# Router logits of the second half from un-normalised residual chunks; weight prefetch split around the first gather

## The chip, the cores and the metric

One core of one Trainium2 chip runs the whole program. The metric is the device time of one execution in microseconds (us), median over runs.

## The reference: one layer of a hybrid decoder

1024 prompt rows and 8 x 4 sample rows of width D = 1024 go through adaLN-modulated RMSNorm, a combined input projection, three mixers, an output projection with a gated residual add, and then a mixture of experts (32 experts, two for each row). Cut to what matters here:

```
x  = x + g1 * mixed                                   # mixed: the output projection's product
h2 = rms_norm(x, norm2_g) * (1 + sc2) + sh2           # A2 = norm2_g * (1 + sc2), B2 = sh2
g_logits = h2 @ w_router_g + b_router_g               # 4 groups
e_logits = h2 @ w_router_e + b_router_e               # 32 experts
# top-1 group, top-2 experts in it; rows sorted by expert, padded to blocks of 128
y = sum of weight * (silu(h2 @ w1[e]) * (h2 @ w3[e])) @ w2[e]
out = rms_norm(x + g2 * y, final_norm_g)
```

The prompt rows share one A2 and one B2, each sample sequence has its own. With r the inverse root mean square of a row, h2 @ W = r * ((x * A2) @ W) + B2 @ W.

## The kernel before: two halves, a routing step, 33 expert blocks

**Dense stage.** Rows are worked in two halves, g = 0 (512 prompt rows) and g = 1 (512 prompt rows and 32 sample rows, five tiles t = 0 to 4). PE's products are *items* (`item(g, i, ...)`), one for each 128 columns of output, with three f32r matmuls for each 128 rows of weights (high by high, low by high, high by low). The last eight items of a half are the output projection (`out_item`). Each gives 128 columns of the result with tokens along the free dimension; `out_transpose` turns them back, and DVE's `out_add` adds them to the residual `xres`.

**Order.** All of it is written out by hand: each engine has one program, with semaphores between them. Nothing is scheduled by a tool.

**The tail of half 0** is woven into half 1: `tail_h2(0, t)` on DVE makes h2 rows, PE transposes them (`h2_transpose`), ACT copies (`tail_tile`), PE's `logits` multiplies eight chunks by the router's 36 columns.

**The tail of half 1** stands by itself, since nothing dense is left: DVE waits for ACT's sums of squares of all eight chunks (`x1_sq`), makes r (`tail_start`), and makes h2 of the five tiles; for each tile PE transposes eight chunks (`last_transpose`), ACT copies them (`last_tile`), PE multiplies (`last_logits`), DVE adds the bias. GpSimd (POOL) writes rows of x1 and h2 to DRAM through its own queue. 44 matmuls on `ident` whose result nobody reads run ahead of it on PE.

**Routing** (`moe_vector`, `moe_tensor`) is a chain of small DVE instructions on the logits. `oh_ok` says that the experts are chosen; PE's rank matmuls follow (behind 30 matmuls of `keep_busy`), then DVE makes the list of rows of each expert (`tok_ok`), and POOL gathers the first block of h2 rows out of DRAM (`gather(0)`).

**Experts.** 33 blocks (`NB`), each of 128 gathered rows. A block takes six weight chunks of 1 MB (`CHUNKS`: four of w1 and w3, two of w2), which SP loads into a ring of `RN` = 13 buffers. ACT rounds a chunk (`high`, `whr`), DVE makes the rest (`low`, `wl`), PE multiplies (`up`, `Y`); `T` transposes gathered rows, `G` the hidden ones. ACT applies a sigmoid (`sigm`), and DVE two products (`gate_one`, `gate_two`). Load n waits until chunk n - 13 has been multiplied (`m_c`). `dense_done` holds an engine until all the dense stage's rows are in DRAM; SP, POOL, ACT and DVE each wait there.

Of the kernel before, what the change touches and what calls it, by code (L numbers as in the profile page):

```python
# [74 lines left out]
N_CONST = 14  # L75
# [3 lines left out]
def build(nc, x_prompt, x_sample, c_prompt, c_sample, state_conv_a, state_conv_c, norm1_g, norm2_g,  # L79
# [5 lines left out]
    with ctx:  # L85
# [7 lines left out]
        y_dram = nc.dram_tensor("y_rows", (2 * TPAD, D), F32, kind="Internal").ap()  # L93
        table = nc.dram_tensor("slot_table", (NBLK * P * NE, 1), I32, kind="Internal").ap()
# [60 lines left out]
        w_hi = [sb(f"w_hi{s}", [P, KD, P], F32R) for s in range(WS)]  # L155
        a_in = sb("a_in", [P, CW, HA + HALF + NS * AS])
# [10 lines left out]
        cv_end = top[0]  # L167
        p_in = sb("p_in", [P, HC + HALF + NS * CS])
# [9 lines left out]
        wsT = sb("wsT", [P, HEADS, P])  # L178
        wsS = sb("wsS", [SMP, HEADS, SMP])
        s_bias = sb("s_bias", [P, CW, P])  # L180
# [19 lines left out]
        rw = sb("rw", [P, KD, NR])  # L200
        rb = sb("rb", [P, NR])
        assert top[0] <= nc.sbuf_usable_end, top[0] - nc.sbuf_usable_end

        h2s, h2T, sqd = [None] * (PT + 1), [None] * 2, [None] * 2
        h2s[0], o = at("h2s0", [P, D], F32, act0_at)
        h2T[0], o = at("h2T0", [P, KD, P], F32, o)
        A2, o = at("A2", [P, D], F32, o)
# [4 lines left out]
        h2T[1], _ = at("h2T1", [P, KD, P], F32, macc_at)  # L212
# [14 lines left out]
        sp8, o = at("sp8", [P, PT + 1, KD], F32, vT_at)  # L227
# [109 lines left out]
        id_ok, sz_ok, az_ok, wsr_ok = (sem(n) for n in ("id_ok", "sz_ok", "az_ok", "wsr_ok"))  # L337
# [4 lines left out]
        x0_in = [sem(f"x0_in{t}") for t in range(PT)]  # L342
# [18 lines left out]
        vT_ok, vn_ok, v_out = sem("vT_ok"), sem("vn_ok"), sem("v_out")  # L361
# [8 lines left out]
        h2_last = [sem(f"h2_last{s}") for s in range(2)]  # L370
        ab_in, abs_in = sem("ab_in"), sem("abs_in")
        h2_ok, h2_out, x1_out = sem("h2_ok"), sem("h2_out"), sem("x1_out")
        hT_ok, hT_rd, lg_ok, lg_rd = sem("hT_ok"), sem("hT_rd"), sem("lg_ok"), sem("lg_rd")
# [22 lines left out]
        def lg_bank(t):  # L396

            return (q[1], z[1])[t % 4 // 2][:, t % 2, :]
# [45 lines left out]
        for g in range(2):  # L444
            if g:
                for i in range(PT):
                    use(0, "h2T", 0, i), use(1, "lg", 0, i)
# [4 lines left out]
            if g:  # L452
                use(0, "stA"), use(1, "stC")
            for c in range(CW):
                use(c % 2, "mu", g, c)
            use(1, "var", g)
            for c in range(CW):
                use(c % 2, "bc", g, c)
# [5 lines left out]
        use(0, "h2T", 1), use(1, "lg", 1)  # L464
# [53 lines left out]
        def x_dump(g):  # L518
# [3 lines left out]
        xs_s = conv_flat[0:SMP, :]  # L522
# [13 lines left out]
        m_T, m_xT, m_xl, m_sg, m_g1, m_g2, m_G, m_gT, m_gl, m_y = (  # L536
            sem(n) for n in ("m_T", "m_xT", "m_xl", "m_sg", "m_g1", "m_g2", "m_G", "m_gT", "m_gl", "m_y"))
        o_i, o_w, o_c, o_x, o_sc = (sem(n) for n in ("o_i", "o_w", "o_c", "o_x", "o_sc"))
        f_in = [sem(f"f_in{s}") for s in range(NT)]
# [3 lines left out]
        f_rows = [P] * (NT - 1) + [SMP]  # L543

# [15 lines left out]
        def dense_done(eng):  # L560

            eng.wait_ge(item_mm, 2 * NI)
            eng.wait_ge(h2_last[0], 16 * ((PT + 2) // 2))
            eng.wait_ge(h2_last[1], 16 * ((PT + 1) // 2))
            eng.wait_ge(x1_out, 16 * NT)
            eng.wait_ge(x1_sq, PT + KD * (PT + 1))
            q_wait_read(eng, "lg", 1)
# [21 lines left out]
        def moe_sync(sp):  # L589
# [7 lines left out]
            for n in (0, 1, 2, 3, 8):  # L597
                load(n, CHUNKS[n][0])
            dense_done(sp)
            for n in (4, 5, 6, 7, *range(9, 10 * RN)):  # L600
                load(n, CHUNKS[n][0])
# [39 lines left out]
            for t in F_ORDER:  # L641
                for k in range(2):
                    r0 = t * P + k * TPAD
                    sp.dma_start(yin[0:f_rows[t], t, k, :], y_dram[r0:r0 + f_rows[t], :]).then_inc(f_in[t], 16)
# [6 lines left out]
        def moe_gpsimd(pool):  # L651
            dense_done(pool)
            pool.memset(xg[0][:], 0.0).then_inc(xg0_ok, 1)
            pool.drain()
            pool.memset(xg[1][:], 0.0).then_inc(xg0_ok, 1)
# [1093 lines left out]
        def _(dve):  # L1749
# [557 lines left out]
            for t in range(PT):  # L2307
                tail_h2(1, t)
# [367 lines left out]
```

## Time and profile before

| | us |
|---|---|
| median of 3 runs | 1684.01 |
| lowest and highest run | 1677.58, 1684.67 |
| profiled execution | 1686.75 |
| its span | 1685.0 |
| mean granted clock of TensorE | 0.974 of full speed |

The span is what the trace covers; 1.75 us of the profiled execution lie outside it. Times in the rows below count from the span's start. PE is the matmul engine, DVE the vector engine, ACT the scalar engine, SPq the queue of SyncE that issues loads. A chain step is `start us, duration us, what`, where `what` is the engine, the tile written and the line.

### The profile page before, as it was taken

Reading aid. Unit: us, or ns where it says so; the run is one execution under the profiler, and the core shown is the slowest. Engines: PE = TensorE matmul, PEld = TensorE weight load, DVE = VectorE, ACT = ScalarE, POOL = GpSimd, SP = SyncE. Lnnn points to the kernel's source line nnn. Section 1 sums busy time; section 2 is a strip of 40 time slices with the busy share of each in tenths; the row PEclk is TensorE's granted clock in tenths of the full one; section 3 lists DMA queues with packets and bytes.
Section 4 is the critical chain, followed back from the end, with each engine's and each line's share of the span. In section 5 each row is a group of like instructions: output and inputs, shape, how many; then the busy total and the mean of one; then the engine's idle time right before and its main releaser. Section 6 shows DMA issues by size and latency. Waiting matters only on the chain.

```text
span 1685.0 us, 23762 instructions
## 1 busy us (share of the span) xinstructions
PE 1606.8 (95%) x9382; PEld 1386.0 (82%) x9382; DVE 1259.1 (75%) x1691; ACT 805.0 (48%) x875; POOL 244.7 (15%) x239
## 2 busy tenths in 40 slices
PE   5999999999999999999999998999999999999953
PEld 3776788788789999999999996888888888888841
DVE  3668886756839798967454268989989999899847
ACT  4222232244432223222333434887878878878722
POOL 2310000000000000002002012355321221212200
PEclk9999999999999999999999978999999999999987
DMA  9965223424434322324134347999999999999865
GB/s 340 303 201 158 78 88 89 137 76 144 128 99 147 91 86 69 97 79 133 58 94 131 152 175 236 409 390 398 383 379 377 384 367 388 375 388 395 308 231 191
DMA packets 215761, 368.51 MB, mean 219 GB/s; under 512 B 15110, under 2 KB 163654, under 8 KB 190298
## 3 DMA queue, kind: packets, MB, share of 16 engines
q1 hardware_dynamic: 197724, 327.95, 55.1%
q0 software_dynamic: 17280, 36.89, 6.1%
q10 hardware_dynamic: 646, 2.15, 0.3%
q8 instruction: 75, 1.23, 0.3%
q14 instruction: 36, 0.29, 0.0%
HBM read 353.45 MB, written 31.20 MB: 228 GB/s over the span
## 4 chain that ended last, share of the span: by engine, by line
PE 85%; DVE 7%; DMA 2%; DVEq 2%; issue 1%; ACT 1%; POOL 0%; SPq 0%; POOLq 0%; ACTq 0%
PE z L2428 15%; PE z L2430 15%; PE z L2429 15%; PE z L723 7%; PE z L725 7%; PE z L724 7%; PE z L740 4%; PE z L742 4%; PE z L741 4%; PE q L714 2%; PE q L2321 1%; DMA ada_h<-in_w_ada_dram 1%; PE q L2340 1%; PE q L731 1%; DVE conv L1919 1%
## 5 line engine op out<-in xcount | busy, mean ns | idle before, releaser
L973 DVE TENSOR_TENSOR wl<-wr,whr 128x2048 fp32r<-128x2048 f32 x198 | 444.2, 2284 | 0.0
L2428 PE MATMUL z<-h_hi,w_hi 128*128 128x272 f32 (+1 forms) x1248 | 410.2, 329 | 2.7 <-issue 1.2
L2430 PE MATMUL z<-h_hi,w_lo 128*128 128x272 f32 (+1 forms) x1248 | 404.6, 324 | 0.0
L2429 PE MATMUL z<-h_lo,w_hi 128*128 128x272 f32 (+1 forms) x1248 | 403.9, 324 | 0.0
L881 ACT ACTIVATE whr<-wr 128x2048 fp32r<-128x2048 f32 x198 | 376.3, 1914 | 37.9 <-PE z L725 32.2
L1751 DVE TENSOR_TENSOR w_lo<-w_raw,w_hi 128x1024 fp32r<-128x1024 f32 (+1 forms) x168 | 179.5, 1069 | 143.3 <-ACT w_hi L1483 143.3
L2428 PEld LDWEIGHTS z<-h_hi,w_hi 128*128 128x128 f32 x1248 | 236.8, 190 | 31.9 <-issue 13.7
L2430 PEld LDWEIGHTS z<-h_hi,w_lo 128*128 128x128 f32 x1248 | 236.3, 189 | 17.1
L2429 PEld LDWEIGHTS z<-h_lo,w_hi 128*128 128x128 f32 x1248 | 236.7, 190 | 15.7 <-issue 0.2
L723 PE MATMUL z<-whr,xTh 128*128 128x512 f32 x528 | 209.9, 398 | 2.4 <-DVE xTl L973 2.4
L725 PE MATMUL z<-wl,xTh 128*128 128x512 f32 x528 | 207.1, 392 | 0.0
L724 PE MATMUL z<-whr,xTl 128*128 128x512 f32 x528 | 206.5, 391 | 0.0
L1919 DVE SCALAR_TENSOR_TENSOR conv<-a_in,parT,conv 128x512 f32<-128x512 f32 x360 | 193.7, 582 | 14.1 <-issue 0.9
L1483 ACT ACTIVATE w_hi<-w_raw 128x1024 fp32r<-128x1024 f32 (+1 forms) x168 | 150.3, 929 | 46.0 <-DMA w_raw<-in_w_in_dram 45.9
L1652 ACT ACTIVATE sig<-z 128x512 f32<-128x512 f32 (+1 forms) x48 | 29.3, 611 | 287.6 <-PE z L2430 287.6
L669 POOL DMA_INDIRECT y_rows<-ysb,tb x32 | 93.2, 2911 | 392.0 <-ACT ysb L873 392.0
L723 PEld LDWEIGHTS z<-whr,xTh 128*128 128x128 f32 x528 | 100.2, 190 | 22.4 <-DVE xTl L973 2.8
L725 PEld LDWEIGHTS z<-wl,xTh 128*128 128x128 f32 x528 | 99.7, 189 | 21.4
L724 PEld LDWEIGHTS z<-whr,xTl 128*128 128x128 f32 x528 | 99.9, 189 | 19.8
L740 PE MATMUL z<-whr,gTh 128*128 128x512 f32 x264 | 105.8, 401 | 0.4 <-DVE gTl L973 0.4
L742 PE MATMUL z<-wl,gTh 128*128 128x512 f32 x264 | 103.1, 391 | 0.0
L741 PE MATMUL z<-whr,gTl 128*128 128x512 f32 x264 | 103.0, 390 | 0.0
(378 smaller groups left out, 2240.8 us busy)
## 6 DMA issues: line engine op xcount, KB each, us to landing
wr<-in_w_dram SPq DMA_DIRECT2D x198, 1024.0 KB, 7.9
w_raw<-in_w_in_dram SPq DMA_DIRECT2D x104, 512.0 KB, 3.8
ada<-in_w_ada_dram SPq DMA_DIRECT2D x6, 2048.0 KB, 14.2
w_raw<-in_w_branch_dram SPq DMA_DIRECT2D x48, 256.0 KB, 2.7
w_raw<-in_w_out_dram SPq DMA_DIRECT2D x16, 512.0 KB, 3.8
yin<-y_rows SPq DMA_DIRECT2D x16, 512.0 KB, 10.0
ada_h<-in_w_ada_dram SPq DMA_DIRECT2D x2, 2048.0 KB, 15.2
ada_u<-in_w_ada_dram SPq DMA_DIRECT2D x2, 2048.0 KB, 10.0
```

Of the source, the lines that this page charges most:

```text
L723: pe.matmul(out, xTh[s][:, k, :], hi[:, i * FF:(i + 1) * FF], start=(k == 0), stop=False)
L724: pe.matmul(out, xTl[s][:, k, :], hi[:, i * FF:(i + 1) * FF], start=False, stop=False)
L725: last = pe.matmul(out, xTh[s][:, k, :], lo[:, i * FF:(i + 1) * FF], start=False, stop=(k == KD - 1))
L740: pe.matmul(out, gTh[:, k, :], hi[:, w0:w0 + 512], start=(k == 0), stop=False)
L742: last = pe.matmul(out, gTh[:, k, :], lo[:, w0:w0 + 512], start=False, stop=(k == KF - 1))
L881: act.activation(whr[n % HN][:], wr[n % RN][:], ACT.Copy).then_inc(m_hi, 1)
L973: return dve.tensor_tensor(out, a, b, op)
L1751: return dve.tensor_tensor(out, a, b, op)
L1919: last = dve.scalar_tensor_tensor(out, x, wt, out, ALU.mult, ALU.add)
L2428: pe.matmul(out, w_hi[w][:, k, :], hi[:, k, t0:t1], start=(k == 0), stop=False)
L2429: pe.matmul(out, w_hi[w][:, k, :], lo[:, k, t0:t1], start=False, stop=False)
L2430: last = pe.matmul(out, w_lo[w][:, k, :], hi[:, k, t0:t1], start=False, stop=(k == kn - 1))
```

## The change

Nine things are done.

1. The logits of half 1 are no longer taken from h2. PE transposes chunks of `xres` as each becomes ready (`x1_columns`), ACT multiplies by A2 (a column) while copying, and PE multiplies the router's columns (padded to 64) as the stationary side by 512 rows at once (`x1_scores`); even chunks write PSUM partitions 0 to 63, odd ones 64 to 127. `last_rows` turns the result back and adds the two halves. DVE multiplies by r and adds a bias that includes B2 @ W (`last_scores`). The samples go the same way in small (`sample_scores`).
2. The h2 rows of half 1 are made in place in `xA` (= xres * A2, made by `x1_scale` between the output items): three tiles by DVE, and the last prompt tile and the sample tile by PE (`h2_product`), read by ACT.
3. The eighth chunk's squares move from ACT to DVE; the other seven are taken before the last item ends.
4. `out_transpose(1, 3, 0)` moves into the middle of the last output item, and the 44 idle matmuls go; `keep_busy` ahead of the rank goes from 30 to 26.
5. SP writes x1 and h2 of half 1, in place of POOL. Its h2 writes wait until its x1 writes have landed.
6. The weight chunks: 0 to 4 are loaded early, where it was 0 to 3 and 8; then 5, 6 and 12 when the last item is done; 7 to 11 wait for the first gather to land, where eight chunks were issued at `dense_done`.
7. Half 0's logits are made by the same method in one go (`first_columns`, `first_rows`) in place of four times eight products.
8. `factor_columns`, `shift_scores` and `shift_rows` bring A2 as columns and B2 @ W, in half 1's dense stage.
9. Experts: Silu on ACT and one DVE product (`gate`) take the place of the sigmoid and two products. DVE no longer waits at `dense_done`, but for `he_ok` behind `oh_ok`.

The core of the diff:

```diff
@@ moe_sync
-            for n in (0, 1, 2, 3, 8):
+            for n in range(5):
                 load(n, CHUNKS[n][0])
+            sp.wait_ge(item_mm, 2 * NI)
+            for n in (5, 6, 12):
+                load(n, CHUNKS[n][0])
+            sp.wait_ge(xa_ok, KD)
+            for t, rows in tiles(1):
+                r0 = (PT + t) * P
+                sp.dma_start(x1_dram[r0:r0 + rows, :], xres[0:rows, t, :]).then_inc(last_out[t % 2], 16)
...
             dense_done(sp)
-            for n in (4, 5, 6, 7, *range(9, 10 * RN)):
+            sp.wait_ge(m_xg[0], 16)
+            for n in (7, 8, 9, 10, 11, *range(13, 10 * RN)):
                 load(n, CHUNKS[n][0])
@@ moe_tensor
-            keep_busy(pe, 30)
+            keep_busy(pe, 26)
             s = q_wait_free(pe, "rank")
+            pe.wait_ge(he_ok, PT + 1 - NH_D)
@@ moe_vector
-            dense_done(dve)
...
             last.then_inc(oh_ok, 1)
+            dve.wait_ge(he_ok, PT + 1 - NH_D)
...
-            def gate_one():
-                tt(gs[:], hsg[:], z[0][:, 0, :], ALU.mult).then_inc(m_g1, 1)
-
-            def gate_two():
-                tt(gs[:], gs[:], z[0][:, 1, :], ALU.mult).then_inc(m_g2, 1)
+            def gate():
+                tt(gs[:], hsg[:], z[0][:, 1, :], ALU.mult).then_inc(m_g2, 1)
@@ scalar engine, end of the dense stage
+            q_wait_read(act, "mc")
+            for c in range(KD):
+                x1_read(c)
+            x1_read_samples()
+            scores_read(1)
+            act.wait_ge(r_ok, 1)
+            for t, rows in tiles(1)[NH_D:]:
+                act.activation(hdg[0:rows, t - NH_D, 0:rows], ident[0:rows, 0:rows], ACT.Copy,
+                               scale=r2y[0:rows, t:t + 1]).then_inc(hd_ok, 1)
+            for t, rows in tiles(1)[NH_D:]:
+                act.wait_ge(xc_ok, KD + 1 + t - NH_D + 1)
+                act.activation(xA[0:rows, t, :], h2_bank(t)[0:rows].rearrange("p b c -> p (b c)"), ACT.Copy).then_inc(he_ok, 1)
@@ vector engine, end of the dense stage
             tail_start(1)
-            for t in range(PT):
-                tail_h2(1, t)
-            dve.wait_ge(abs_in, 16 * 2 * NS)
-            tail_h2(1, PT, SMP, (xs_s[:, D:2 * D], xs_s[:, 0:D]))
-            for t, rows in tiles(1):
-                tail_logits(1, t, rows)
+            for t in range(NH_D):
+                dve.scalar_tensor_tensor(xA[:, t, :], xA[:, t, :], r2y[:, t:t + 1], B2[:], ALU.mult, ALU.add).then_inc(h2_ok, 1)
+            last_scores()
@@ tensor engine
+            def column_scores(out, x, c, first, last):
+
+                r = 64 * (c % 2)
+                return pe.matmul(out[r:r + NRP], rw[:, c, :], x, start=first, stop=last)
...
+            def h2_product(t, rows):
...
+                for h in range(2):
+                    out, cc = h2_bank(t)[0:rows, h, :], slice(512 * h, 512 * h + 512)
+                    pe.matmul(out, ident[0:rows, 0:rows], shift[0:rows, cc], start=True, stop=False)
+                    last = pe.matmul(out, hdg[0:rows, t - NH_D, 0:rows], xA[0:rows, t, cc], start=False, stop=True)
```

PE before, behind the last output item (`ot` is the output item's result, `h2s` the h2 rows, `h2T` their transposes, `rw` the router's columns):

```order
L2321 MATMUL q<-ident,ot_110 128x128 x4
L2321 MATMUL q<-ident,ot_110 32x128
L2321 MATMUL q<-ident,ot_111 128x128 x4
L2321 MATMUL q<-ident,ot_111 32x128
L2644 MATMUL z<-ident 128x128 x44
L2321 MATMUL q<-ident,h2s_141 128x128 x8
L2321 MATMUL z<-ident,h2s_148 128x128 x8
L2473 MATMUL q<-rw,h2T_142 128x36 x8
L2321 MATMUL q<-ident,h2s_149 128x128 x8
L2473 MATMUL q<-rw,h2T_147 128x36 x8
```

The same place in the changed kernel, from the first transposes behind the last item to the matmuls ahead of the rank (`x1T` are the transposed chunks, `LT` the logits with tokens along the free dimension, `both` a matrix that adds the halves, `B_148` the shift B2):

```order
L2449 MATMUL q<-ident,xres 128x128 x8
L2573 MATMUL z<-x1T,rw 64x512 x2
L2449 MATMUL z<-ident,xres 128x128 x8
L2449 MATMUL q<-ident,xA 128x32 x8
L2573 MATMUL z<-x1T,rw 64x512 x4
L2573 MATMUL z<-x1T,rw 64x32 x8
L2577 MATMUL q<-both,LT_143 128x36 x4
L2577 MATMUL q<-both,LT_143 32x36
L2645 MATMUL z<-B_148,ident 128x512
L2646 MATMUL z<-xA,hdg 128x512
L2645 MATMUL z<-B_148,ident 128x512
L2646 MATMUL z<-xA,hdg 128x512
```

The transposes of h2 and the 36-column products are gone; chunks of `xres` are transposed instead, and products for h2 rows now stand behind the logits.

SP in the changed kernel, from the last of the five early chunks on, with the semaphores that it waits for:

```order
L621 DMA wr_193<-in_w_dram 128x2048
L621 DMA wr_211<-in_w_dram 128x2048 [waits item_mm]
L621 DMA wr_213<-in_w_dram 128x2048
L621 DMA wr_207<-in_w_dram 128x2048
L639 DMA x_rows<-xres 128x1024 [waits xa_ok]
L651 DMA h_rows<-xA 128x1024 [waits last_out0,last_out1,x1_sq,h2_ok,xc_ok,r_ok]
L651 DMA h_rows<-xA 128x1024 [waits he_ok]
L651 DMA h_rows<-xA 32x1024 [waits he_ok]
L621 DMA wr_215<-in_w_dram 128x2048 [waits h2_ok,he_ok,x1_sq,h2_out,x1_out,lg_rd,last_out1,m_xg0,last_out0,item_mm]
```

Between the weight loads there now stand ten writes of rows; before, SP's list had weight loads alone here, and the writes were in POOL's.

## Rows read from the trace of the kernel before

**Rows 1.** The page's part 4: the chain that ended last, by engine.

```profile
PE 85%; DVE 7%; DMA 2%; DVEq 2%; issue 1%; ACT 1%; POOL 0%; SPq 0%; POOLq 0%; ACTq 0%
```

**Rows 2.** The chain in order of time: from the last output item to block 2.

```profile
968.15 0.14 PE z L2430
969.37 0.79 DVE xres L1751 x2
974.71 0.19 DVE ssq L1965
978.02 1.28 DVE h2s L1941
...
1002.89 0.37 DVE m8g L996 x4
...
1020.80 5.88 DMA xg<-h_rows,tok
1026.93 1.96 PE q L714 x8
...
1031.25 0.79 PE z L723
...
1070.26 0.88 PE q L714 x8
1088.01 0.88 PE q L714 x8
```

**Rows 3.** Stretches: busy us (and instructions) of each engine, granted clock, DMA share.

```profile
970.00:972.00 2.00, 1.79 (x16) 1.78 (x17) 1.83 (x5) 1.81 (x13) 0.00 (x0) 1.00 0.00 0
986.00:988.00 2.00, 2.00 (x11) 2.00 (x11) 1.93 (x2) 0.00 (x0) 0.94 (x2) 0.50 0.97 377
1006.00:1008.00 2.00, 2.00 (x21) 2.00 (x19) 1.74 (x12) 2.00 (x2) 0.00 (x0) 1.00 1.00 414
1200.00:1300.00 100.00, 100.00 (x473) 83.77 (x473) 90.84 (x56) 80.28 (x57) 24.33 (x12) 1.00 0.99 377
```

**Rows 4.** Timeline of PE from the last item to the rank.

```profile
970.21 0.77 PE L2321 MATMUL q<-ident,ot 128*128 128x128 f32 x5 [1.39 <-DVE xres L1751]
970.81 9.99 PE L2644 MATMUL z<-ident 128*128 128x128 f32 x88
1002.06 8.79 PE L748 MATMUL z<-ident 128*128 128x128 f32 x60
1011.85 0.18 PE L760 MATMUL q<-ohs,tri 128*128 128x32 bf16 x1 [1.01 <-issue]
```

**Rows 5.** The chain: steps on PE elsewhere.

```profile
50.81 1.85 PE q L2340 x16
322.42 1.72 PE q L2583 x4
350.49 1.90 PE q L2603 x32
522.91 1.71 PE q L2445 x16
```

**Rows 6.** Timeline of ACT: a table load, then rounding of three chunks.

```profile
1010.01 1.28 ACT L889 ACT_TABLE_LOAD   x1
...
1011.44 5.49 ACT L881 ACTIVATE whr<-wr 128x2048 fp32r<-128x2048 f32 x3
```

**Rows 7.** Groups of instructions from 900 to 1055 us: count, busy, mean ns.

```profile
L1751 DVE TENSOR_TENSOR xres<-q,xres 128x512 f32<-128x512 f32 x8 | 5.4, 669 | 0.0
```

**Rows 8.** DMA issues from 905 to 1060 us: KB each, median us to landing.

```profile
wr<-in_w_dram SPq DMA_DIRECT2D x21, 1024.0 KB, 9.7
h_rows<-h2s POOLq DMA_DIRECT2D x4, 512.0 KB, 4.5
```

**Rows 9.** Gathers of rows (tile xg) from 1000 to 1100 us.

```profile
DMA to landing us min/median/max: 4.1/5.9/11.9
```

**Rows 10.** Waits in SP's queue from 1100 to 1600 us: total us, times, longest.

```profile
SPq L587 <- PE z L725: 272.3, 109, 2.9
```

More of the change, by code:

```diff
@@ L341, in build @@
         bada_in = [sem(f"bada_in{s}") for s in range(2)]
-        x0_in = [sem(f"x0_in{t}") for t in range(PT)]
+        rows_in = [sem(f"rows_in{t}") for t in range(NT)]
         x_in = [sem(f"x_in{s}") for s in range(5)]
@@ L2411, in _, with item @@
             pe.wait_ge(xt_free, PT)
-            def item(g, i, hi, lo, split_ok=None):
+            def item(g, i, hi, lo, split_ok=None, between=None):
                 u, s, w, kn = i // 2, i % 2, (NI * g + i) % WS, w_cols(i)
@@ L2421, in item @@
                     [(part, k) for part in parts for k in range(kn)]
-                for (b, t0, t1), k in steps:
+                for n, ((b, t0, t1), k) in enumerate(steps):
+                    if between and n == kn:
+                        between()
                     out = z[s][:, b, 0:t1 - t0]
@@ L2477, in out_item, with row_scores, first_columns @@
-            def out_item(g, j, s):
+            def column_scores(out, x, c, first, last):
+                r = 64 * (c % 2)
+                return pe.matmul(out[r:r + NRP], rw[:, c, :], x, start=first, stop=last)
+            def row_scores(out, g, t, rows):
+                return pe.matmul(out[0:rows, t * NR:(t + 1) * NR], LT[g][:, t * P:t * P + rows], both[:], start=True, stop=True)
+            def first_columns():
+                pe.wait_ge(consts, N_CONST)
+                pe.wait_ge(par2_in, 16 * N_PAR2)
+                q_wait_read(pe, "h2T", 0, PT - 1)
+                q_wait_free(pe, "vT", 1, 0)
+                for c in range(KD):
+                    last = column_scores(q[1][:, 0, :], h2T[:, c, :], c, c < 2, c >= KD - 2)
+                last.then_inc(lt_ok, 1)
@@ new lines, in first_rows, with x1_columns @@
+            def first_rows():
+                pe.wait_ge(ltc_ok, 1)
+                for t in range(PT):
+                    last = row_scores(q[1][:, 1, :], 0, t, P)
+                last.then_inc(lg_ok, 1)
+            def x1_columns(c):
+                pe.wait_ge(xa_ok, c + 1)
+                if c == 0:
+                    q_wait_read(pe, "oT", 1, KD - 2)
+                elif c == 1:
+                    pe.wait_ge(z_free[1], NI)
+                elif c == 3:
+                    q_wait_read(pe, "oT", 1, KD - 1)
+                elif c >= 5:
+                    pe.wait_ge(xe_ok, c - 4)
+                for t in range(PT):
+                    last = transposed(x1_bank(c)[:, t * P:(t + 1) * P], xres[:, t, c * P:(c + 1) * P])
+                last.then_inc(xc_ok, 1)
@@ new lines, in factor_columns, with shift_scores @@
+            def factor_columns():
+                s = q_wait_free(pe, "mc")
+                pe.wait_ge(mc_in, 32)
+                transposed(q[s][:, 0, 0:P], bn_g[:, 0:P])
+                transposed(q[s][:, 0, P:9 * 2 * KD], bn_g[0:2 * KD, P:2 * P]).then_inc(q_ready[s], 1)
+            def shift_scores():
+                s = q_wait_free(pe, "sc")
+                q_wait_read(pe, "mc")
+                for c in range(KD):
+                    last = column_scores(q[s][:, 0, 0:9], abT[:, :, 0, c], c, c < 2, c >= KD - 2)
+                last.then_inc(q_ready[s], 1)
@@ L2638, in _ @@
                     out_transpose(g, j - 1, 1)
-                    out_item(g, j, 1)
-                if g:
-                    out_transpose(g, KD // 2 - 1, 0)
-                    out_transpose(g, KD // 2 - 1, 1)
-            for _ in range(44):
-                pe.matmul(z[1][:, 0, 0:P], ident[:], ident[:], start=True, stop=True)
-            for t, rows in tiles(1):
-                last_transpose(t, rows)
-                if t:
-                    last_logits(t - 1, P)
-            last_logits(PT, SMP)
+                    if g and j == KD // 2 - 1:
+                        out_item(g, j, 1, between=lambda: out_transpose(1, KD // 2 - 1, 0))
+                    else:
+                        out_item(g, j, 1)
+            x1_columns(0)
+            out_transpose(1, KD // 2 - 1, 1)
+            for c in (1, 2, 3):
+                x1_columns(c)
+            x1_scores(0)
+            x1_columns(4)
+            x1_columns(5)
+            x1_scores(1)
+            x1_columns(6)
+            x1_columns(7)
+            x1_samples()
+            x1_scores(2)
+            x1_scores(3)
+            sample_scores()
+            last_rows()
+            for t, rows in tiles(1)[NH_D:]:
+                h2_product(t, rows)
             moe_tensor(pe)
```

412 lines of the change are left out of this document (259 added, 153 removed).

## The prediction

> **What bounds the kernel now.** I read the chain that ended last first: PE has 85% of it, DVE 7% [rows 1]. Then the chain in order of time. An expert block starts each 17.75 us (1088.01 - 1070.26), and in such blocks PE is busy 100 of 100 us at full clock, DVE 90.8, ACT 80.3 [rows 2, 3]. So the experts are bound by PE, the change gives PE no less to do there, and what it saves on DVE (one product a block) lies beside PE's work: nothing. The dense stage is PE's too. The place where the engines take turns lies between them: the last dense matmul ends at 968.3 (I call this E), the chosen experts are looked for from 1002.89, the first gather is issued at 1020.80, its transposes begin at 1026.93, the first expert matmul at 1031.25 [rows 2]. From E to T(0) that is 58.6 us, while an expert's matmuls need 17.75 us a block; what shortens these 58.6 us comes off the end, as all behind stays in order.
>
> Where they go: E to r ready (978.02), 9.7 us; h2, transposes and logits of five tiles to 1002.89, 24.9 us; routing to the gather 17.9 us; the gather 5.9 us [rows 2]. In the second piece PE worked at half its clock: granted 0.50 from 986 to 988, busy 2.00 of 2 us, after 1.00 at 970 to 972 and again at 1006 to 1008 [rows 3].
>
> **The change, step by step, in us after E, at full clock.** Three chains have to be followed.
>
> *Logits by way of DVE.* DVE is free of the output at +1.1 (969.37) and PE's five transposes take 0.8 (they waited for DVE's earlier sums before, which now come earlier) [rows 2, 4]: +1.9. The sum over four tiles and the samples' own, two instructions at or below 0.67 [rows 7]: +2.8. The eighth chunk's squares, now on DVE: product, reduction and their sample parts, four instructions by 0.67 at most, with the x1 scale ahead, I take 2.2: +5.0. From there to the rows of h2 it took 3.3 (974.71 to 978.02) [rows 2]: +8.3. The last x1 scale 0.7, then three of the four-column kind of instruction that took 1.28 [rows 2]: +12.8. The bias and r on the logits, five small ones, no row: between 0.5 and 2, I take 1.0, as they are far smaller than the 0.67 ones: **+13.8**, where 1002.89 was +34.6.
>
> *Logits by way of PE.* Transposing eight chunks of four tiles is 32 transposes; 16 f32 instructions of a similar size take about 1.9 at most [rows 5], so 3.6; five for the output 0.8; samples and the small products about 2.4. The eight products of 512 columns have no row. A 128-wide one cost 0.86 (four instructions, two products, 1.72); with four strips side by side an instruction cost 0.116 (1.85 / 16), and with two strips, 128 columns, 0.059 (1.90 / 32), against 0.114 (9.99 / 88) for the full width [rows 4, 5]. So two strips run beside each other: 0.43 each, bounds 0.23 and 0.86, the sum 3.4 (1.9 to 6.9). With the wait for the output at the start PE ends the logits at about +11.5, behind DVE's rows only: DVE decides. At 0.86 each PE ends at +15, and all below is 2 us later.
>
> *PE on to the rank.* Behind the logits stand the h2 products of two tiles, eight by 0.86 (the sample tile has 32 rows, but the same 512 columns): 6.9, +18.4. 26 idle matmuls are 52 instructions by 0.114: 5.9, so the rank can start at **+24.3**. DVE reaches the rank's input 9.0 us after its start (1011.85 - 1002.89), +22.8 [rows 2, 4]. So PE is 1.5 us late there, of which DVE hides about 0.4. From the rank to the transposes it was 15.1 (1026.93 - 1011.85). The gather took 5.9 while weight loads filled the DMA (share 1.00 at 1006); the quickest of the gathers took 4.1 [rows 3, 9]. Nothing is loaded now ahead of it, so I take 1.8 off; the bounds are 0 and, if the shortest one still met others, 3. T(0) is then at 24.3 + 15.1 - 0.4 - 1.8 = **+37.2**, where it was +58.6: 21.4 less.
>
> *Rows in DRAM and ACT behind them.* ACT still waits for all rows in DRAM, then needs 5.5 for three chunks, a table load of 1.3 with three small ones, and 5.5 again, say 12.8, before it takes T(0)'s result [rows 6]. SP: three chunks (3 MB; some 380 GB/s, [rows 3]) to about +9, x1 rows 2.1 MB to +14.5, and only then h2. The last tile is read at +19.5 and lands by +23 (a row write took 4.5 [rows 8]). ACT is through at +36, T(0) is done at +39. It fits by 3 us. If the landing is 4 us later, ACT sets the pace.
>
> *What is held back.* Chunks 7 to 11 start when the gather lands. A load lands 9.7 after issue in this stretch [rows 8] and the next follow at 2.8 (1.05 MB at 377 GB/s): 7 at T(0) + 10, then 13, 16, 19, 21. Before, PE's first block took until about T(0) + 19, and chunk 7 is multiplied in the second. In steady blocks SP waits for PE 109 times from 1100 to 1600 us, 272 us in all [rows 10], so there is room to catch up. Nothing.
>
> *The dense stage.* Half 0's logits cost 4 x 1.71 [rows 5]; now eight by 0.43 and four small ones of 0.2 each, 4.3: -2.5. A2's columns and the shift's logits: about 1.7, and 0.4 for a bank that ACT must read first. The transposes inside the last item: +0.6. Sum +0.2, bounds -2 and +4.
>
> **The clock** is what I know least. PE goes without ordinary matmuls from E to about +3.4: transposes and waits alone. Before, the clock held over the pause at 970 (idle 1.39, then 1.00) but then fell and stayed at 0.50 while PE was busy with transposes and products of 36 columns, and it rose within 4 us of ordinary matmuls (1002.06 to 1006) [rows 3, 4]. So a fall near +4 is likely, and the products of 512 columns may lift it again; I take half-speed for 3.5 us, that is 1.7 lost. The Trainium skill, "TensorE: Matmul & The Clock Gate", Part 4, says that a PE transpose does not count as PE being busy. By that rule the clock stays low until the products of 512 columns weigh more than the transposes, which is the second rival below; the trace agrees in so far as the clock stayed at 0.50 where half of PE's work was transposes, but its other half was of 36 columns, so it can't tell the two apart.
>
> **The sum:** -21.4 + 1.7 + 0.2 = -19.5. The profiled execution (1686.75, span 1685.0) would become 1667.2. It lies 2.7 above the median of the runs, so I set the difference against the median: 1684.0 - 19.5 = **1664.5**.
>
> **Rivals.**
>
> *Clock low up to the h2 products.* PE's logits after +4 then take twice as long: about +17.3 (some of it is waiting, which the clock doesn't stretch), DVE +18.4; the products, low for their first 3.9, take 8.9, +26.2; 5.9 idle ones, rank at +32; T(0) at +44.9. Saved 13.7, time **1670.5**. For it: [rows 3]'s 0.50. Against: here products of 512 columns stand in between, from +3.4 on. 22%.
>
> *Clock low all the way, or rows late in DRAM.* Logits +20.3 to +21.4, products 13.8, idle ones 11.8: rank at +46, T(0) at about +59. Time **1684**; or, at full clock, h2 landing 10 us later, which puts ACT at +46: 1674. For the clock: nothing shows that f32 products with 64 of 128 columns used lift it. Against: in [rows 4], [rows 3], f32 matmuls on `ident` did lift it, and the h2 products are as wide. 13% for this group, a third of it within 0.5%, or 8.4 us, of no change, which is about what a measurement of this kernel can tell.
>
> *Slower: Silu brings table loads into each block.* A load costs 1.28 [rows 6]. If Silu and the copies of rounding don't share a table, two loads stand in each block, 2.56 us. ACT has 3.5 us to spare in a block of 17.75 (80.3 of 100), but hidden rows, rounded chunks and T's result all pass through it in turn, so a part shows on PE. It decides above 19.5 / 32 = 0.6 us a block; one load shown is 41 us, time **1705**. Against: at 1010.01 one load stood ahead of the exponential, and the three copies behind it had none [rows 6]. 5%.
>
> *Nothing gained,* since a new wait takes it back (the bank of `mc`, chunks too late, or DVE's waits): **1682**, 7%.
>
> **How the numbers follow.** Forecast 50% (own range 1658 to 1668), first rival 22%, second 13%, Silu 5%, nothing 7%, and 3% for more gain than 27 us, if PE is warm when the first block starts. Range **1657 to 1677**: it leaves out the 5, the 7, the 3 and part of the 13. Faster by over 0.5%: 50 + 22 + 3 + some 8 of the 13 = 0.83. Within 0.5%: 0.11. Slower: 0.06.
>
> **What would show it.** The choice of experts begins at E + 14 (over + 18: the clock; look at the granted clock from E to + 12). The rank starts at + 24 and waits for PE's idle matmuls, not DVE. The gather takes 4.1 or less. ACT is through with its sixth chunk ahead of T(0). Expert blocks keep 17.75 us, without a table load in them, and no ACT wait for chunks 7 to 11. Wrong it would be if ACT or `he_ok` ends the wait at the rank or at T(0), or if the blocks lengthen.

## The result, and the profile of the changed kernel

The changed kernel took 1669.35 us (median of 5 runs, 1666.21 to 1672.21) where the kernel before, on the same chip, took 1679.51 (5 runs, 1677.58 to 1684.67): ratio 0.9936, 95% interval 0.9912 to 0.9960. Five later runs of it had a median of 1669.43. Forecast was 1664.5 in 1657 to 1677, and "faster". So the sign and the range held, but of a gain of 19.5 us only 10.2 came.

The chain by engine, from the page, to be held against [rows 1]: PE has a point more, DVE a point less.

```profile
PE 86%; DVE 6%; DMA 2%; DVEq 2%; ACT 1%; issue 1%; POOL 0%; SPq 0%; POOLq 0%; ACTq 0%
```

The chain in order of time between the last dense matmul and block 2, which answers to [rows 2]. E, the end of the last dense matmul, is 969.2 here.

```profile
970.60 0.75 PE q L2449 x5
...
977.71 1.89 PE z L2573 x8
...
981.53 1.06 PE z L2645 x2
...
989.12 8.83 PE z L803 x52
999.10 0.46 DVE oh L1030
...
1006.37 5.41 DMA xg<-h_rows,tok
...
1012.03 1.96 PE q L769 x8
...
1016.34 0.79 PE z L778
...
1055.27 0.88 PE q L769 x8
1073.02 0.88 PE q L769 x8
```

The reader sees that DVE's long turns of before ([rows 2], 974.71 to 1002.89) are out of the chain, and that PE holds it from 971 to 998. T(0), the first transpose of gathered rows, is at E + 42.8 (1012.03) and was at E + 58.8 (the forecast's 58.6 counts from another end of the same matmul, see the table below). The blocks behind still lie 17.75 us apart.

PE's timeline from E to the rank, to be held against [rows 4]:

```profile
972.95 1.08 PE L2573 MATMUL z<-x1T,rw 128*64 128x512 f32 x4
...
980.27 1.26 PE L2577 MATMUL q<-both,LT 128*128 128x36 f32 x10 [0.26 <-ACT LT L1619]
981.47 1.13 PE L2645 MATMUL z<-B,ident 128*128 128x512 f32 x2
...
985.10 1.04 PE L2645 MATMUL q<-xs_s,ident 32*32 32x512 f32 x2
...
987.70 1.42 PE L2646 MATMUL q<-xA,hdg 32*32 32x512 f32 x2
989.05 8.90 PE L803 MATMUL z<-ident 128*128 128x128 f32 x52
997.78 0.18 PE L816 MATMUL q<-ohs,tri 128*128 128x32 bf16 x1
```

The logits end at E + 12.3, the h2 products at E + 19.9, and then come the 52 instructions of `keep_busy`, at 0.171 us each instead of 0.114. The stretches say why, the granted TensorE clock being the third number from the end (columns as in [rows 3]):

```profile
970.00:972.00 2.00, 1.40 (x13) 1.39 (x13) 0.82 (x3) 1.00 (x3) 0.37 (x1) 1.00 0.78 217
986.00:988.00 2.00, 2.00 (x6) 0.51 (x5) 1.77 (x12) 0.23 (x1) 0.00 (x0) 1.00 0.03 8
990.00:992.00 2.00, 2.00 (x12) 2.00 (x11) 1.64 (x8) 0.17 (x1) 0.00 (x0) 0.50 1.02 395
1006.00:1008.00 2.00, 2.00 (x20) 2.00 (x20) 1.75 (x2) 2.00 (x2) 1.63 (x1) 1.00 0.00 0
1018.00:1020.00 2.00, 2.00 (x6) 1.52 (x6) 1.83 (x7) 0.00 (x0) 0.00 (x0) 0.50 1.00 416
1200.00:1300.00 100.00, 100.00 (x472) 83.71 (x471) 87.80 (x51) 81.34 (x56) 21.01 (x12) 1.00 0.98 376
```

The clock stayed at full through the logits, fell to half (1.2 of 2.4 GHz) only at 988.2, in the last of the products of the sample tile, which use 32 rows and 32 columns of the array, and again under the first block, behind PE's pause at the gather. In the steady stretch DVE lost the 3 us in 100 that the second product cost (90.84 in [rows 3]), and PE's 100 of 100 shows that this is worth nothing.

ACT waits for the rows of h2 and then rounds, beside [rows 6]:

```profile
995.71 5.51 ACT L937 ACTIVATE whr<-wr 128x2048 fp32r<-128x2048 f32 x3 [5.54 <-DMA h_rows<-xA]
...
1001.43 1.28 ACT L945 ACT_TABLE_LOAD   x1
...
1002.86 5.50 ACT L937 ACTIVATE whr<-wr 128x2048 fp32r<-128x2048 f32 x3
```

It is through at 1008.4, 3.7 us ahead of T(0).

### The profile page after: what moved, and what is told of

Its sections match the earlier page's. It is cut to its first block, busy times and chain, and to the rows that moved or that the text cites. A ratio compares the mean times of both kernels' runs of the same rounds, so it can differ in the third digit from the quotient of the medians.

```text
span 1670.5 us, 23444 instructions
## 1 busy us (share of the span) xinstructions
PE 1595.8 (96%) x9246; PEld 1362.9 (82%) x9246; DVE 1243.1 (74%) x1666; ACT 807.9 (48%) x876; POOL 216.0 (13%) x236
## 4 chain that ended last, share of the span: by engine, by line
PE 86%; DVE 6%; DMA 2%; DVEq 2%; ACT 1%; issue 1%; POOL 0%; SPq 0%; POOLq 0%; ACTq 0%
PE z L2558 15%; PE z L2560 15%; PE z L2559 15%; PE z L778 7%; PE z L780 7%; PE z L779 7%; PE z L795 4%; PE z L797 4%; PE z L796 4%; PE q L769 2%; PE q L2449 1%; DMA ada_h<-in_w_ada_dram 1%; PE q L2468 1%; PE q L786 1%; DVE conv L1994 1%
## 5 line engine op out<-in xcount | busy, mean ns | idle before, releaser
L937 ACT ACTIVATE whr<-wr 128x2048 fp32r<-128x2048 f32 x198 | 376.4, 1914 | 38.4 <-PE z L780 32.6
L724 POOL DMA_INDIRECT y_rows<-ysb,tb x32 | 78.2, 2443 | 418.0 <-ACT ysb L929 418.0
```

What stands on the lines that cost most here:

```text
L937: act.activation(whr[n % HN][:], wr[n % RN][:], ACT.Copy).then_inc(m_hi, 1)
```

## Experiments

All edits are to the changed kernel, where nothing else is said. Ratios are to the kernel before, run on the same chip; the changed kernel's own is 0.9936. Most edits are smaller than what runs of one kernel differ by, so the traces are set side by side first, and each is read from its own E:

| trace | E | rank, from E | gather, us | T(0), from E | 2nd block, from E |
|---|---|---|---|---|---|
| before | 968.1 | 43.7 | 5.88 | 58.8 | 71.2 |
| b1, before again | 965.5 | 43.7 | 6.13 | 59.0 | 71.4 |
| b2, before again | 965.6 | 36.0 | 7.05 | 52.3 | 64.1 |
| e8, before, loads held | 965.6 | 36.0 | 5.57 | 50.8 | 63.2 |
| changed | 969.2 | 28.6 | 5.41 | 42.8 | 55.5 |
| a1, changed again | 968.6 | 25.4 | 5.56 | 39.8 | 52.0 |
| e1 | 969.2 | 25.0 | 5.44 | 39.3 | 52.0 |
| e2 | 969.0 | 22.9 | 5.49 | 38.4 | 49.5 |
| e3 | 966.7 | 27.0 | 7.80 | 43.6 | 56.0 |
| e4 | 970.0 | 27.0 | 5.50 | 41.3 | 53.6 |
| e5 | 966.9 | 23.0 | 5.50 | 37.5 | 50.1 |
| e6 | 969.0 | 23.0 | 5.62 | 37.6 | 46.7 |
| e7 | 966.9 | 25.4 | 5.52 | 39.7 | 50.9 |
| e9, e6 again | 969.3 | 23.0 | 5.54 | 37.5 | 46.6 |

(Rank: its first matmul starts. Gather: its step in the chain. T(0): first transpose of gathered rows. 2nd block: the first transpose of its rows. E, the end of the last dense matmul, is taken here as the start of its row in the timeline and 0.13 us, the distance at which such matmuls follow each other; the row's own end, 968.3 in before, lies 0.15 later, and the forecast's 58.6 counts from there.)

**e1: the sample tile's products over the whole array.** Its rows of h2 are left out.

```diff
-out = h2_bank(t)[0:rows, h, :]
-pe.matmul(out, ident[0:rows, 0:rows], shift[0:rows, cc], ...)
-pe.matmul(out, hdg[0:rows, t - NH_D, 0:rows], xA[0:rows, t, cc], ...)
+out = h2_bank(t)[:, h, :]          # for t == PT
+pe.matmul(out, ident[:], B2[:, cc], ...)
+pe.matmul(out, ident[:], B2[:, cc], ...)
```

> The changed kernel, but the four matmuls that make the sample tile's h2 rows (32 rows and 32 columns of the array, 512 moving columns) are replaced by four of 128 rows and 128 columns with the same 512 moving columns, on other data; the h2 rows of the samples are therefore left out of the result, the logits are as before. Theory A: the granted clock falls to 0.50 behind the logits (989 to 995 in the changed kernel) because the sample tile's product leaves most of the array idle. Then the clock stays at 1.00 through this stretch, the 52 idle-matmul instructions ahead of the rank take about 5.9 us in place of 8.8, the rank starts about 3 us sooner after the last dense matmul, and so does the first expert transpose, unless the rows' landing holds it. Rival C: the fall comes from the transposes and waits right behind the dense stage, late by some delay; then the low stretch stays and nothing moves.

Measured: 1667.66 (1666.63 to 1668.61), ratio 0.9922 (0.9896 to 0.9948). PE's timeline in e1:

```profile
987.56 1.02 PE L2652 MATMUL q<-B,ident 128*128 128x512 f32 x2
988.42 5.97 PE L803 MATMUL z<-ident 128*128 128x128 f32 x52
994.22 0.18 PE L816 MATMUL q<-ohs,tri 128*128 128x32 bf16 x1
```

The 52 idle instructions take 5.97 us, which is the forecast's 5.9, and the rank stands at E + 25.0. With as many products of as many columns, spread over the whole array, the clock stayed up in this trace. That doesn't yet show that the small ones make it fall: a1 below has the small ones and no fall either, so this single trace decides neither for theory A nor against rival C.

**e2: four idle matmuls instead of 26.**

```diff
-            keep_busy(pe, 26)
+            keep_busy(pe, 4)
```

> The changed kernel with 4 idle matmuls ahead of the rank in place of 26. Theory A: PE holds the rank (DVE sat idle 5.5 us for it in the changed kernel), so the rank starts as soon as the experts are chosen, 5 to 5.5 us sooner, and the first expert matmul 4 to 5.5 us sooner; total 4 to 5 us less than the changed kernel, less what a lower clock at the first blocks costs (up to 2). Rival B: the landing of the h2 rows and ACT's six roundings behind it set the first block; ACT was through at 1008.4 and took the first transposes' result at 1014.0, so then the gain ends at 5.6 minus the sooner rank, or stops outright if the gather itself waits for the rows: at most 1 to 2 us.

Measured: 1665.78 (1665.17 to 1666.53), ratio 0.9913 (0.9887 to 0.9939). PE's timeline:

```profile
988.97 2.07 PE L803 MATMUL z<-ident 128*128 128x128 f32 x8
991.98 0.18 PE L816 MATMUL q<-ohs,tri 128*128 128x32 bf16 x1 [0.94 <-DVE ohs L1088]
...
993.61 5.56 PE L803 MATMUL z<-ident 128*128 128x128 f32 x28
```

The rank now waits for DVE, at E + 22.9; the forecast had DVE there at + 22.8. So PE held the rank, and neither ACT nor the landing of h2 did. The clock is low here too, so the next 28 idle instructions take 5.56 instead of 3.39, and part of the 5.7 us is given back.

**e3: chunks 7 to 11 not held for the gather.**

```diff
-            sp.wait_ge(m_xg[0], 16)
```

> The changed kernel, but weight chunks 7 to 11 are loaded once all rows are in DRAM, without waiting for the first gather. My forecast took 1.8 us for the emptier DMA during the gather; the profile of the changed kernel shows 5.41 where it was 5.88. If contention costs what the two profiles show, the gather's step in the chain is 5.4 to 6 us here and the total differs by under 1 us. Rival: the hold is what keeps the gather quick, and without it the gather step grows by 1.8 or more and all behind it with it. Chunks 7 to 11 are early in either case.

Measured: 1668.69 (1667.49 to 1671.81), ratio 0.9932 (0.9910 to 0.9954). The chain's row of the gather in e3:

```profile
1002.24 7.80 DMA xg<-h_rows,tok
```

The hold is worth 2.4 us of the gather, and from the rank to T(0) it took 16.6 us where it was 14.3. The medians (0.7 us apart, and not the way of the trace) can't show it: five runs of either kernel lie 4 to 6 us apart, and this trace's own E is 2.5 us earlier.

**e4: SP writes h2 without waiting for x1 to land.**

```diff
-            sp.wait_ge(last_out[0], 16 * ((PT + 2) // 2))
-            sp.wait_ge(last_out[1], 16 * ((PT + 1) // 2))
```

> The changed kernel, but SP writes the h2 rows without first waiting until its x1 writes have landed. Theory: that wait held the h2 writes from 981 to 988 (issue at 988.0) and all rows' landing to 995.7; without it the landing comes at 992 to 993 (the sample tile is read by ACT at 990.2), ACT is through with six chunks at about 1005.5, and since nothing of this is on the chain (the rank is), the first expert matmul and the total stay within 1 us. Rival B: the landing is on the chain by way of ACT or of the gather; then the first block starts about 3 us sooner.

Measured: 1668.04 (1666.74 to 1672.24), ratio 0.9931 (0.9909 to 0.9954). ACT's rounding:

```profile
993.66 5.51 ACT L935 ACTIVATE whr<-wr 128x2048 fp32r<-128x2048 f32 x3 [3.10 <-DMA h_rows<-xA]
```

It begins at E + 23.7 where it was E + 26.5, and T(0) did not follow: from the rank to T(0) it took 14.3 us in both. The rows' landing is not on the chain there.

**e7: the sigmoid and two products back in the blocks.** The waits that go with them, and the place of the two products in DVE's order, change too and are left out here.

```diff
-act.activation(hsg[:], z[0][:, 0, :], ACT.Silu)...
+act.activation(hsg[:], z[0][:, 0, :], ACT.Sigmoid)...
-tt(gs[:], hsg[:], z[0][:, 1, :], ALU.mult)...
+tt(gs[:], hsg[:], z[0][:, 0, :], ALU.mult)...
+tt(gs[:], gs[:], z[0][:, 1, :], ALU.mult)...
```

> The changed kernel with the expert blocks of before: a sigmoid on ACT and two products on DVE. Forecast: nothing, as a block stays 17.75 us with DVE at 90 of 100 us. Rival: the one product less on DVE was on the chain in the first two blocks, and the total grows by 0.7 to 1.4 us (too small for the total, but the distance from the first block's transposes to the third's shows it).

Measured: 1669.94 (1664.97 to 1670.88), ratio 0.9948 (0.9933 to 0.9964). From T(0) to the fourth block it took 41.9 us, in the changed kernel 43.1 (85.9 - 42.8) and in a1 42.8. The trace gained 1.2 rather than lost, at the first block's clock; the medians can't be told apart. Behind the first block, where the clock is full in all traces, there is a small difference: from the second block's transposes to the fourth's it took 30.72 to 30.75 us in the five traces with the sigmoid (before, b1, b2, e8, e7) and 30.41 to 30.60 in the nine with Silu. So Silu gives 0.1 to 0.3 us once, less than the expectation's rival had, and nothing that the times can tell. It brought no table loads: one load stands in the first block of either.

**b1 and b2: the kernel before, unchanged, once each; a1: the changed kernel again.**

> The kernel before, unchanged, for a second trace. Its profiled execution had a span of 1685.0 us at a mean granted clock of 0.974, while most of its other runs lie at 1677 to 1680 with 0.978 to 0.982. Theory: the 14.5 us between the two profiles and the 10 us between the medians differ because in the first trace PE spent longer at half clock in the stretch behind the dense stage or in the prologue; a trace of a run near 1678 then shows the routing's start some microseconds sooner after the last dense matmul, or the last dense matmul itself sooner. Rival: the expert blocks differ in period. They would then not be 17.75 us in the new trace.

b1 took 1684.46, so it could not test its expectation, which needed a run near 1678. Its tail was that of the first trace (T(0) at E + 59.0), and from that came the theory written down for b2, that the runs differ in the dense part.

> The kernel before, unchanged, once more, for its chance from run to run. Theory (its runs differ in the dense part, by the granted clock, not behind it): T(0) again at E+58.6 to 59.1, blocks 17.75 us apart, and the span differs from 1682.7 and 1685.0 only by where E lies (965.5 and 968.1). Rival (they differ in the tail between E and T(0)): T(0) more than 1 us off that distance.

b2 took 1677.46, with T(0) at E + 52.3: its theory falls and the rival holds, and with it what b1's expectation had said of a run near 1678. Two traces with the same E, 965.5 and 965.6, differ by 6.7 us at T(0). The stretches of b1:

```profile
976.00:980.00 4.00, 3.19 (x28) 2.85 (x26) 3.85 (x4) 0.78 (x1) 1.07 (x2) 1.00 0.16 63
980.00:984.00 4.00, 3.38 (x26) 3.41 (x27) 3.92 (x4) 1.27 (x2) 1.79 (x4) 0.86 0.96 368
984.00:988.00 4.00, 4.00 (x22) 4.00 (x20) 3.85 (x6) 1.02 (x1) 1.35 (x3) 0.50 0.99 387
...
996.00:1000.00 4.00, 4.00 (x31) 3.85 (x31) 0.51 (x4) 0.00 (x0) 0.04 (x1) 0.50 0.01 4
```

and of b2:

```profile
976.00:980.00 4.00, 3.27 (x29) 2.93 (x27) 3.85 (x4) 0.69 (x1) 1.07 (x2) 1.00 0.14 56
980.00:984.00 4.00, 3.30 (x30) 3.33 (x31) 3.92 (x4) 1.36 (x2) 1.71 (x4) 1.00 0.96 369
984.00:988.00 4.00, 4.00 (x40) 4.00 (x38) 3.85 (x5) 1.99 (x2) 1.44 (x3) 1.00 0.98 385
...
992.00:996.00 4.00, 4.00 (x23) 4.00 (x23) 3.29 (x35) 3.60 (x2) 0.96 (x1) 0.57 0.68 213
996.00:1000.00 4.00, 4.00 (x39) 4.00 (x38) 3.61 (x32) 2.49 (x5) 0.00 (x0) 1.00 0.93 320
```

With the same work on PE up to 980, the clock fell to half near 983 in b1, and stayed there past 1002; in b2 it fell only at 992, for less than 4 us. Of 51 runs of the kernel before in this study, b1 and b2 among them, 40 lie between 1676.46 and 1680.17 and 11 between 1684.01 and 1686.62, with none between. The two traced runs of it with the long low stretch took 1684.46 and 1686.75, the one with the short 1677.46. That this stretch makes the two groups is shown for these three and inferred for the rest.

> The changed kernel, unchanged, in more runs. Theory (the half-clock stretch behind E is what makes runs of both kernels differ; before has it at 18 us or at 3, the changed kernel at 3 to 6): the profiled run has E at 966 to 970, T(0) at E+39.5 to E+43, the runs fall in 1665 to 1672 without a second group, the median is 1669 and 0.6% under before's. Rival (the changed kernel has a second group too, at 1675 or more, not met in its five runs): such runs appear.

a1: 1669.43 (1667.43 to 1671.48, 5 runs), ratio 0.9946 (0.9932 to 0.9959). PE in a1:

```profile
987.08 1.02 PE L2646 MATMUL q<-xA,hdg 32*32 32x512 f32 x2
988.03 6.07 PE L803 MATMUL z<-ident 128*128 128x128 f32 x52
```

The same products as in the changed kernel's first trace, and no fall behind them. That part of a1's expectation held, and no second group appeared: the ten runs of the changed kernel lie between 1666.21 and 1672.21.

**e8: the kernel before with the hold alone** (chunks 4, 5, 12 at `dense_done`, the others after the gather).

```diff
-            for n in (4, 5, 6, 7, *range(9, 10 * RN)):
+            for n in (4, 5, 12):
+                load(n, CHUNKS[n][0])
+            sp.wait_ge(m_xg[0], 16)
+            for n in (6, 7, 9, 10, 11, *range(13, 10 * RN)):
```

> The kernel before with only one part of the change: behind the last dense product SP issues chunks 4, 5 and 12 alone, and 6, 7, 9, 10, 11 and the rest after the first gather has landed. Theory (the hold is worth what the gather gains and nothing else): the gather's step in the chain goes from 5.88 us to 5.4, as in the changed kernel, T(0) comes at E+58.3 where before had 58.8, nothing in the first blocks waits for a chunk, and the median is within 0.2% of before. Rival 1 (contention takes more when the loads run): the step falls by 2.4 us, the distance between the changed kernel with and without the hold, and T(0) comes at E+56.4. Rival 2 (held chunks are late once the tail is long): a first block waits on a weight load, and the kernel is slower.

Measured: 1678.25 (1674.95 to 1684.83, 12 runs), ratio 0.9993 (0.9976 to 1.0011): no change. The rank and the gather start within 0.01 us of each other in b2 and e8; the gather of b2, and behind it that of e8:

```profile
1010.53 7.05 DMA xg<-h_rows,tok
```

```profile
1010.52 5.57 DMA xg<-h_rows,tok
```

T(0) comes 1.5 us earlier and the second block 0.9. The step had three lengths in the traces of before, so the hold shortened it by 0.3 (5.88), 0.6 (6.13) or 1.5 us (7.05): the theory's 0.5 lies in that span, the first rival's 2.4 does not, and the median can't resolve any of them. The absolute E + 58.3 of the expectation missed, since this trace had the short low stretch. Two of the 12 runs lie at 1684.7 and 1684.8, so the second group is there as well.

**e5: the sample tile's h2 on DVE, PE's products all full width, 14 idle matmuls.** The order of SP's writes follows, and as in e4 SP doesn't wait for x1 to land.

```diff
-NH_D = 3
+NH_D = 2
-            keep_busy(pe, 26)
+            keep_busy(pe, 14)
-            for t, rows in tiles(1):
+            for t in (0, 1, PT, 2, 3):
+dve.scalar_tensor_tensor(xA[0:SMP, PT, :], xA[0:SMP, PT, :], r2y[0:SMP, PT:PT + 1], xs_s[:, 0:D], ...)
```

> The changed kernel, complete, with the h2 rows split otherwise: DVE makes tiles 0 and 1 and the sample tile, PE tiles 2 and 3 (both with all 128 rows and columns of the array); 14 idle matmuls ahead of the rank; SP's h2 writes don't wait for x1. Theory A (the sample tile's product lowers the clock, and PE holds the rank): the clock stays at 1.00 up to the rank, PE is ready for it at about 23 us after the last dense matmul, where DVE is too, the first expert transposes come at + 37 to + 38 in place of + 42.8, total 5 us less than the changed kernel, 1664 to 1665. Rival B: the rows' landing (at + 22 to + 24) and ACT's 12.7 us behind it become the bound: ACT takes the transposes at + 39 at the earliest only if the landing slips beyond + 26; then the gain is 2 to 3.

Measured: 1664.90 (1664.36 to 1666.16), ratio 0.9919 (0.9905 to 0.9932). The rank stands at E + 23.0, T(0) at E + 37.5. The three edits were not taken apart; e2, with fewer idle matmuls alone, had the rank at E + 22.9 too, at half clock, and T(0) at E + 38.4.

**e6, and e9 the same again beside a1: e5 with idle matmuls ahead of the first block as well.**

```diff
+            keep_busy(pe, 8)      # behind the positions' product
+                keep_busy(pe, 10) # behind T(0)
```

> The run before this one in the list, with 8 idle matmuls more while PE waits for the experts' list, and 10 more between the first block's transposes and its first product. Theory: the clock falls to 0.50 over PE's waits there (1012 to 1022 in the changed kernel), which costs 0.9 us on the transposes and 0.2 us on each of some 12 products; kept busy it stays at 1.00, and the first block is 2.5 to 3.5 us shorter, of which DVE's rounding, next in line, leaves 1 to 2 us in the total. Rival: DVE's roundings set the first two blocks whatever PE's clock, so the second block's transposes come no sooner after the first's; total unchanged.

> The version with the sample tile's products on DVE and with idle matmuls ahead of the first block once more, beside the changed kernel on the same chip. Theory: no half-clock stretch from E to the first block, T(0) at E+37.6, the second block's transposes 9.1 us behind T(0), runs within 2 us of each other, the median 5 to 6 us under the changed kernel's. Rival (the four runs of before were good ones by chance): the median is within 3 us of the changed kernel's.

Measured: 1663.19 (1662.49 to 1663.93), ratio 0.9905 (0.9890 to 0.9920); again, on another chip, 1662.73 (1661.42 to 1663.46, 4 runs), ratio 0.9904 (0.9889 to 0.9919), where a1 had 1669.43: 6.7 less, a little over the 5 to 6 expected. The first block of e6 in the chain, and its clock:

```profile
1006.60 1.14 PE q L770 x8
...
1010.10 0.50 PE z L779
```

```profile
1012.00:1014.00 2.00, 2.00 (x10) 1.63 (x10) 1.83 (x7) 0.75 (x1) 0.00 (x0) 1.00 0.99 412
```

The eight transposes take 1.14 us instead of 1.96, the first product 0.50 instead of 0.79, and the second block follows T(0) by 9.1 us instead of 12.7 (12.3 in a1). Against e5 the second block comes 3.4 us sooner in the traces (E + 46.7 for E + 50.1), and the medians differ by 1.7 (1664.90 to 1663.19), with the runs of the two not overlapping: the 1 to 2 us that the theory left in the total, and against the rival. It is the best version here, 1.0% under the kernel before.

## Why the forecast was right and where it was not

**DVE's half** held: the choice of experts starts at 983.02 (E + 13.8 forecast and measured), from this row of DVE's timeline:

```profile
983.02 0.71 DVE L1052 MAX8 m8g<-gpad 128x8 f32<-128x8 f32 x9
```

The same row of b2, a run of the kernel before that loses little to the clock, is at E + 27.0:

```profile
992.62 0.71 DVE L996 MAX8 m8g<-gpad 128x8 f32<-128x8 f32 x9
```

**PE's logits**: forecast E + 11.5, measured + 12.3. The unseen product, put at 0.43 with bounds 0.23 and 0.86, took 0.46 (3.65 / 8) in half 0:

```profile
563.68 3.65 PE L2573 MATMUL q<-h2T,rw 128*64 128x512 f32 x16
573.41 0.98 PE L2577 MATMUL q<-both,LT 128*128 128x36 f32 x8
```

Two strips do run beside each other, in f32 too.

**The rank** was forecast at E + 24.3 and came at + 28.6, in a1 at + 25.4. Without a fall, in a1, 0.8 of the 1.1 us are the logits. The term that was off is the clock: "a fall near +4 is likely" and "half-speed for 3.5 us, that is 1.7 lost". No trace of the changed kernel has a fall at + 4, though PE had nothing but transposes and 64-column products there. It fell, where it did, at + 19 to + 20, at or behind the sample tile's products, and in the first trace it added 2.9 us to the idle matmuls' 5.9. The forecast weighed a rule of the Trainium skill, "TensorE: Matmul & The Clock Gate", Part 4 (a transpose does not count as PE being busy), and read it so that the clock would be low among the logits. It was 1.00 in every stretch from 970 to 988, so the measurement goes against that reading; what transposes alone would do, no run here shows. (The half of PE's work that the forecast gives to transposes in the kernel before is a count: by time they were 1.95 of 5.2 us a tile.) And the first rival, the clock low up to the h2 products, gave 1670.5, near the result, for a reason that did not occur.

**The gather**: "the quickest of the gathers took 4.1 ... so I take 1.8 off". With nothing else loading it took 5.41 to 5.62 in ten traces (e8 and nine of changed forms). The transfer is not all of it: from 1006 to 1008 no byte moves, and POOL is busy for 1.63 us. POOL's rows of the changed kernel show more:

```profile
1006.37 2.28 POOL L720 DMA_INDIRECT xg<-h_rows,tok  x1 [9.68 <-DVE tok L1126]
1008.96 1.02 POOL L720 DMA_INDIRECT xg<-h_rows,tok  x1 [0.30 <-issue]
```

The first gather's instruction takes 2.28 us on POOL (2.27 in before), the next one's 1.02. The difference is 1.3 us, as much as the forecast missed this step by, though no run shows that it is the cause. So the 4.1 of [rows 9], the shortest of several, was no price for the first gather, and 0.5 came, not 1.8. The Trainium skill, "DMA: Bandwidth & Descriptors", section "Anatomy of one DMA — SWDGE (gpsimd) path", has a fit of 2.0 us and the bytes over 436 GB/s; an estimate by it for these 524 KB is 3.2, and the traces show 5.4. The hold does keep the gather from becoming longer: 7.80 in e3.

**From the rank to T(0)** the forecast had 12.9 (15.1 - 0.4 - 1.8), the traces 14.3 (997.78 to 1012.03; e1 14.3): all but 0.1 is the gather. That a1's T(0), at + 39.8, lies within 0.9 of the forecast's 38.9 (37.2 and the 1.7 for the clock) is in part luck: 1.1 too little at the rank and 1.5 behind it stood against the 1.7 for a fall that did not come.

**ACT and the rows**: forecast through at + 36, measured + 39.2 (1008.4), as the rows landed at + 26.5 instead of + 23. It ends 3.7 us ahead of T(0) in the first trace, and 0.2 ahead in e1 (1002.82 + 5.49 against 1008.50), with 2.0 more until T(0)'s result is there to be taken. So it held, with little room once PE is quicker; e5 and e6, which are, also write h2 without SP's wait.

**The blocks** held: 17.75 us (1055.27, 1073.02), one table load in the first and none after, no wait of ACT for a chunk. The rivals with table loads (1705) and with nothing gained (1682) fell.

**The dense stage**: forecast + 0.2. By the time of the same instructions in b2 and in the changed kernel: from the dense matmul at 361.6 (364.6) to that at 635.0 (635.4), half 0's logits between them, 273.4 became 270.8 (-2.6, forecast -2.5); the stretch with A2 and the shift's logits 86.6 became 88.8 (+2.2, forecast +2.1); the last item 6.1 became 6.7 (+0.6, as forecast). To that come 0.5 for the products of `shift_rows`, which make B2 @ W's rows (PE's timeline, 810.06 to 810.65) and which the forecast had in its 2.1. The sum is +0.7, forecast +0.2. But E came 3.6 later, and the rest is elsewhere: 1.4 up to 323 us, and 1.6 from 323 to 363, where the granted clock is 0.96 in b2 and 0.91 in the changed kernel. The four traces of the kernel before had 0.96 (three) and 1.00 in this stretch; the ten of changed forms had 0.91 (six), 0.96 (two) and 1.00 (two). Whether the change makes the 0.91 likelier is open and wasn't tried.

**The sum, and the step that failed.** The traces of before and after differ by 14.5 us: E +1.1, E to T(0) -16.0, behind it +0.4. But the step "T(0) ... was +58.6: 21.4 less", and after it "I set the difference against the median: 1684.0 - 19.5", took the profiled execution for the usual one. It is the unusual one: [rows 3]'s 0.50 at 986 was there in both traces of the 1684 group (11 of 51 runs), and not in b2, of the larger group. Two of the three runs shown ahead of the forecast were of the smaller group. Against b2 the forecast comes out so: spans 1674.9 and 1666.3 (a1), -8.6, which is the forecast -19.5, + 6.4 since T(0) was at + 52.3 and not + 58.6, + 0.9 since a1's T(0) is at + 39.8 and not + 38.9, + 2.8 for E, + 0.9 behind T(0); the parts sum to -8.5. The mechanism was right and two terms were off: above all what before loses to the clock, 6.4 of the 21.4, and E, 2.8. Of the 12.5 us that a1 gains on b2 from E to T(0), 10.6 are gained at the rank and 1.9 behind it, 1.5 of these by the gather. No run takes the new logits (parts 1 to 3 of the change) out by themselves; that they bring the 10.6 is read from the order of the traces, where the choice of experts starts at E + 27.0 in b2 and at E + 13.8 in the changed kernel. And since the forecast's base lay 4.5 above the later median (1684.0 to 1679.5), half of the miss was hidden by luck: the gain missed by 9.3, the time by 4.9 only.

## What to carry to other kernels

Where a term of the sum is a stretch at half clock, look at the spread of the times first: two groups with nothing between them mean that one trace shows one of two forms, and the saving has to be worked out for each. When other work leaves the chain, what was padding (idle matmuls that keep the clock) becomes the chain; count it anew, and put it where PE really pauses, which brought e6's second block 3.4 us forward and gave 1.7 us in the median over e5. Price a gather by one of the same rows and bytes, not by the shortest in view.

## What the runs showed of the hardware, unexpected

The clock can go either way under the same instructions: in b1 and b2 they agree up to 980, and then one has 0.50 for some 20 us and the other for some 3, which is 6.7 us at T(0). In the changed kernel the same holds for the pair of its first trace and a1, 8.90 and 6.07 us for the same 52 instructions. The place of the fall hardly varied: E + 17.3 in before and b1, E + 26 in b2 and e8, E + 19 to + 20 in the changed forms that had one. f32 products on 32 rows and 32 columns preceded a fall in that trace, in e2, and a shorter one in e3 (7.36) and e4 (7.70), not in a1 or e7: four of six traces. Without them there was none ahead of the rank in four (e1, e5, e6, e9), three of which differ in other things too. Transposes and 64-column f32 products in turn kept the full clock for 13 us, in all ten traces that have them. These counts don't separate a cause from chance, and what decides between the two outcomes is open.
